# Halves of an activation next to each other, a shared last scaling, and reordered beginnings of two attention layers

## The chip, the cores and the metric

The kernel runs on one core of a Trainium2 chip. The metric is the time on the device in microseconds (us): the median of several runs. The kernel before takes 1296.48 us (three runs, 1295.65 to 1296.82). A row of the profile names the engines: PE is TensorE, PEld its weight load, DVE is VectorE, ACT is ScalarE, POOL is GpSimd and SP is SyncE, which issues nearly all DMAs.

## The reference, cut to what matters

Two blocks on 256 tokens of width 1024, in fp32, one after the other. The first has four layers (a0, b0, c0, a1), each of which projects h, mixes tokens, gates, projects back and normalises:

```python
for i in range(DEPTH):                    # 4
    if kind == 0:                         # layers a
        branch = fourier_mix(h)
    elif kind == 1:                       # layer b: grouped-query attention
        q = apply_axial_rope(rms_norm(q, q_norm_g[j]), ang_row, ang_col)
        k = apply_axial_rope(rms_norm(k, k_norm_g[j]), ang_row, ang_col)
        branch = gqa_block_attention(q, k, v)
    else:                                 # layer c: three dilated windows, 16 heads
        qg = apply_rope(qkv[:, :, 0, g], ang_1d)
        kg = apply_rope(qkv[:, :, 1, g], ang_1d)
        og, lg = dilated_group_attention(qg, kg, qkv[:, :, 2, g], dil, window // (2 * dil))
        ...
    mem_out = memory_attention(qm, mk, mv)
    y = jnp.concatenate([branch, mem_out], axis=-1) * jax.nn.silu(gate)
    h = layer_norm(DEEPNORM_ALPHA * h + jnp.matmul(y, w_out[i]), ln_g[i], ln_b[i])
```

The second has two layers (d0, d1) of three mixers and an MLP, and a last norm:

```python
for l in range(DEPTH_2):                  # 2
    x = x + mix @ w_out[l]
    x = x + squared_relu_mlp(rmsnorm(x, norm_mlp_g[l]), mlp_w1[l], mlp_w2[l])
return rmsnorm(x, final_norm_g)
```

## The kernel before, in words

**Products in three parts.** An fp32 product is made of three matmuls on operands that are split into a high part, rounded, and a low part, the rest: high times high, high times low and low times high (mm3, L490 to L492). Activations are held with their features on the partitions: h_hi and h_lo, each 8 tiles (k) of 256 tokens, both in the tile h_both; r_hi and r_lo hold what goes into the projections back. Where a token tile of h is the stationary operand (token_major, chunks of queries and keys, residual), 128 of its columns are loaded and 512 columns of a weight stream. Where a weight is stationary (feature_major, feature_half), 256 tokens of h stream.

**The up products of the MLP (L1500, L1501)** do it in two matmuls: the high weights meet h_hi and h_lo in one matmul of 512 moving columns, and the low weights meet h_hi in one of 256. For each MLP there are 16 units with 16 such pairs, so each line runs 512 times in the kernel. In h_both the low half of a tile k lies 8 KB behind its high half.

**Weights** come in units of up to 1 MB. SP loads a unit into one of three raw slots, ACT rounds it (w_hi, L1603), DVE subtracts (w_lo, L2169), and PE waits for w_lo. There are three split slots, so ACT may round unit u when PE has finished unit u - 3. Which unit ACT and DVE take at which place is fixed by the calls round_weights(key, ahead) and weights(key, ahead): they handle all units up to the one that key's product uses, plus ahead (plus one in ACT's).

**Order.** There is no scheduler at run time: each engine runs the list that its block writes (block.tensor, block.scalar, block.vector, block.sync), and semaphores, wrapped in Steps, tie them together. Every wait is thus in front of all that stands behind it on its engine.

**Layer b, beginning.** PE: chunk 2 (keys and values), chunk 0 (first half of the queries), the memory queries (qm), heads(0), which is pair_scores(0) alone, half a chunk 1, turn_k, heads(1), the other half, gate 4, turn_q(0), and then heads(2), which starts with pair_turned(0). DVE: norms of the keys, rope_k twice, norms of the queries, then the calls that the diff reorders: rope_q rotates 8 heads of a token tile with sines (L2433) and cosines, pair_max(q) takes the row maxima of scores (L2457), for which the exponentials of ACT wait, pair_normal(q) divides by the sums (L2468), and weights(...) splits units. ACT: the exponentials of pair 0, the evacuations of turn_k (L1614), the rounding of the next unit, the exponentials of pair 1, tokens(1) (four reads of chunk 1, L1774 and L1775), two roundings, the silu of gate 4 (L1806), the evacuations of turn_q(0) (L1614), and those of pair_turned(0).

**Layer c, first section.** qk_section(0) has three chunks in six half chunks of one unit and 24 matmuls each. DVE rotates each finished chunk (rope) into the one tile c_rot (a part of prob, L2535), and PE transposes it from there (turn, through banks 3 and 6; the transposes are L578), after which ACT copies it out and DVE may rotate the next. The turns stand in front of half chunks 3 and 5 and in front of the second half unit of v_section(0).

**The end.** The last two products each add a half of a row tile to x (L2651), ACT sums the squares (L1992), rms makes the factor with small DVE instructions, and DVE scales a whole row tile by factor and gain in one instruction (L3023). SP stores a row tile when it is scaled (L1580).

Of the kernel before, what the change touches and what calls it, by code (L numbers as in the profile page):

```python
# [23 lines left out]
F32 = mybir.dt.float32  # L24
# [6 lines left out]
P = 128  # L31
# [119 lines left out]
def build(nc, A, out):  # L151
    _, n_kept = constants()
    with ExitStack() as ctx:
# [7 lines left out]
        h_both = sb("h_both", [P, 2, KT, S], F32R)  # L161
        h_hi, h_lo = h_both[:, 0, :, :], h_both[:, 1, :, :]
# [112 lines left out]
        row_out = Steps("row_out")  # L275
        vector_step = Steps("vector_step")
# [145 lines left out]
        C_TURN_BANK = (3, 6)  # L422
        C_EARLY_BANKS = (0, 1, 2, 4, 5)
# [55 lines left out]
        def _(pe):  # L479
# [264 lines left out]
            for li, (kind, j) in enumerate(LAYERS):  # L744
# [248 lines left out]
                else:  # L993
# [130 lines left out]
                    def qk_section(c):  # L1124
                        for i in range(6):
                            heads("qk", c, i)
                            if i in (3, 5):
                                turn(c, i // 2 - 1)
                            half_chunk(c, i)

                    def v_section(vh, turned, before):
                        for i in range(6):
                            heads("v", vh, i)
                            if i == before:
                                turn(turned, 2)
                            half_values(vh, i)
# [5 lines left out]
                    v_section(0, 0, 1)  # L1142
# [10 lines left out]
                    v_section(1, 2, 1)  # L1153
# [57 lines left out]
            for l in range(2):  # L1211
# [272 lines left out]
                def up(e):  # L1484
                    for u in range(2):
# [7 lines left out]
                        for k0 in range(0, KT, step):  # L1493
                            if e + u == 0:
                                pe.wait_ge(h_ready.sem, h_ready.at(((L, "mlp"), k0 // 2)))
                            for m in range(2):
                                o = bank[2 * u + m]
                                for k in range(k0, k0 + step):
                                    hi, lo = [a[:, k, m * P:(m + 1) * P] for a in w]
                                    nc.tensor.matmul(o, hi, h_both[:, :, k, :], start=k == 0, stop=False)  # L1500
                                    i = nc.tensor.matmul(o[:, 0:S], lo, h_hi[:, k, :], start=False, stop=k == KT - 1)  # L1501
                            if e + u + k0 == 0:
                                stream_tiles((L, "mlp"), (L, "wo"), 1)
# [22 lines left out]
        def _(sp):  # L1526
# [51 lines left out]
            for b in range(NB):  # L1578
                sp.wait_ge(row_out.sem, row_out.at(b))
                sp.dma_start(out[0, b * P:(b + 1) * P, :], z[:, b, :]).then_inc(stored, 16)  # L1580
            sp.wait_ge(stored, 16 * NB)
# [14 lines left out]
        def _(act):  # L1596
# [22 lines left out]
            def hidden_hi(L, nxt, tiles, tiles_there):  # L1619

                for j in range(4):
                    act.wait_ge(tiles_there.sem, tiles_there.at((L, "zt", j)))
                    nc.scalar.activation(flat2(h_hi[:, 2 * j:2 * j + 2, :]), tiles[:, j % 2, :], ACT.Copy)\
                        .then_inc(h_rounded.sem, h_rounded.next((nxt, j)))
# [68 lines left out]
            for j, what in ((1, "scaled"), (0, "hi"), (1, "hi"), (3, "scaled"), (2, "hi"), (3, "hi")):  # L1693
# [6 lines left out]
                else:  # L1700
                    there = tiles_scaled if j % 2 else tiles_read
                    act.wait_ge(there.sem, there.at(("in", "zt", j)))
                    nc.scalar.activation(flat2(h_hi[:, 2 * j:2 * j + 2, :]), tile_place(j), ACT.Copy).then_inc(h_rounded.sem, h_rounded.next(("a0", j)))
# [9 lines left out]
            for li, (kind, j) in enumerate(LAYERS):  # L1713
# [126 lines left out]
                else:  # L1840
# [66 lines left out]
                    def qk_section(c):  # L1907
                        for i in range(6):
                            heads("qk", c, i, turned=(c, i // 2 - 1) if i in (3, 5) else None)

                    def v_section(vh, turned, before):
                        for i in range(6):
                            heads("v", vh, i, turned=(turned, 2) if i == before else None)
# [11 lines left out]
                    v_section(0, 0, 1)  # L1925
# [13 lines left out]
                    v_section(1, 2, 1)  # L1939
# [213 lines left out]
            for n in range(2):  # L2153
                for b in range(NB):
                    act.wait_ge(dve_read.sem, dve_read.at(("d1", "dn", n, b)))
                    half_squares("end", "end", b, n)


        @block.vector
        def _(dve):  # L2160
# [49 lines left out]
            def first_tiles():  # L2210
# [8 lines left out]
                for j in range(4):  # L2219
# [4 lines left out]
                    v.tensor_tensor(flat2(h_lo[:, pair, :]), tile_place(j), flat2(h_hi[:, pair, :]).bitcast(F32), SUB).then_inc(h_ready.sem, h_ready.next(("a0", j)))  # L2224
# [152 lines left out]
            for li, (kind, j) in enumerate(LAYERS):  # L2377
# [33 lines left out]
                elif kind == "b":  # L2411
# [13 lines left out]
                    def rope(b, c0, nh, gain, rot, rs):  # L2425
# [5 lines left out]
                        for r in range(2):  # L2431
                            for f in range(2):
                                tt(r5[:, :, f, r, :], s5[:, :, f, 1 - r, :], t5[:, f, r, :].unsqueeze(1).to_broadcast([P, nh, 16]), MUL)  # L2433
# [48 lines left out]
                    norms(8, 8, ("p", 0), b_sq, "qm")  # L2482
                    rope_q(0, 0)
                    pair_max(0)
                    weights((L, "s", 0, 1))
                    rope_q(0, 1)
                    pair_normal(0)
                    pair_max(1)
                    weights((L, "s", 1, 1))
# [173 lines left out]
            for l in range(2):  # L2663
# [306 lines left out]
                def tile_lo(part, j):  # L2970
# [3 lines left out]
                    v.tensor_tensor(flat2(h_lo[:, pair, :]), split_t[:, j % 2, :], flat2(h_hi[:, pair, :]).bitcast(F32), SUB)\  # L2974
# [41 lines left out]
                for n in range(2 if l == 1 else 0):  # L3016
                    for b in range(NB):
                        add_rows((L, "dn", n, b), n, b, bank[4 + 2 * n + b], factor=S_(10 + b, 1))
                        if n == 1:
                            link(rms("end", "end", b))  # L3020
                            if b == 0:
                                dve.wait_ge(gf_loaded, 16)
                            v.scalar_tensor_tensor(z[:, b, :], x[:, b, :], S_(8 + b, 1), gf, MUL, MUL).then_inc(row_out.sem, row_out.next(b))  # L3023
# [25 lines left out]
```

## Time and profile before

| what | value |
|---|---|
| median of three runs | 1296.48 us |
| the profiled execution | 1295.2 us |
| its span | 1293.4 us |
| PE busy | 1255.6 us (97%) |
| DVE busy | 892.0 us (69%) |
| ACT busy | 704.8 us (54%) |
| matmuls | 7512 |
| L1500 / L1501 | 512 matmuls each, mean 399 / 281 ns |
| from HBM | 194.94 MB, mean 152 GB/s with what is written |

The span is what the profile covers. The execution's time holds 1.8 us more, around it. Busy times of PE add up the durations of matmuls that overlap by their drains, so the distance between two starts tells the rate, and not the duration. An idle time in brackets stands in front of the row's first instruction, with the engine and line that ended it. A row with x8 merges eight instructions.

### The profile page before, as it was taken

How to read it: one execution, taken by the hardware profiler on the slowest of the kernel's cores; microseconds unless marked ns; L12 is line 12 of the kernel's file. 1: busy time of each engine (PE TensorE's matmuls, PEld its weight loads, DVE VectorE, ACT ScalarE, POOL GpSimd, SP SyncE). 2: the span in 40 equal slices, each digit the busy share in tenths (PEclk: the TensorE clock that was granted, in tenths of full speed). 3: DMA queues.
4: the chain of work that ended last, by engine and by line, in shares of the span. 5: the costliest groups of instructions: out<-in, count | busy, mean ns of one | idle time of the engine just before them, and what ended most of it. 6: DMA issues, size and time to landing. Idle time of an engine off the chain costs nothing.

```text
span 1293.4 us, 19153 instructions
## 1 busy us (share of the span) xinstructions
PE 1255.6 (97%) x7512; PEld 1073.4 (83%) x7512; DVE 892.0 (69%) x1602; ACT 704.8 (54%) x1029; POOL 2.4 (0%) x8
## 2 busy tenths in 40 slices
PE   8999999999999999999999999999999999999997
PEld 7997787778888787887998987888888987888885
DVE  6677996685664746547566998766657897766655
ACT  5634577453467565575535676544444676544442
POOL 0000000000000000000000000000000000000000
PEclk9999999999999999999999999999999999999999
DMA  9444532445643335333343454455654544456560
GB/s 275 148 168 140 163 116 82 163 163 163 196 163 114 119 127 163 98 112 125 115 157 109 150 167 134 138 193 191 200 191 131 170 142 136 148 182 209 184 223 32
DMA packets 147054, 197.22 MB, mean 152 GB/s; under 512 B 4732, under 2 KB 102294, under 8 KB 146966
## 3 DMA queue, kind: packets, MB, share of 16 engines
q1 hardware_dynamic: 146838, 195.96, 47.0%
q8 instruction: 60, 0.98, 0.3%
q14 instruction: 28, 0.23, 0.1%
q0 software_dynamic: 128, 0.04, 0.0%
HBM read 194.94 MB, written 1.05 MB: 152 GB/s over the span
## 4 chain that ended last, share of the span: by engine, by line
PE 79%; DVE 12%; ACT 5%; issue 3%; DMA 0%; DVEq 0%; ACTq 0%
PE bank L490 18%; PE bank L492 17%; PE bank L491 17%; PE bank L1500 9%; PE bank L1501 5%; PE bank L578 4%; DVE w_lo L2169 3%; DVE stat L2189 2%; PE bank L1073 1%; PE bank L787 1%; PE bank L691 1%; ACT w_hi L1603 1%; PE bank L1110 1%; DVE stat L2186 1%; DVE arena L2183 1%
## 5 line engine op out<-in xcount | busy, mean ns | idle before, releaser
L2169 DVE TENSOR_TENSOR w_lo<-w_raw,w_hi 128x2048 fp32r<-128x2048 f32 (+5 forms) x190 | 412.9, 2182 | 132.2 <-ACT w_hi L1603 129.5
L1603 ACT ACTIVATE w_hi<-w_raw 128x2048 fp32r<-128x2048 f32 (+5 forms) x190 | 346.3, 1829 | 231.0 <-PE bank L492 157.6
L490 PE MATMUL bank<-w_hi,r_hi 128*128 128x512 f32 (+3 forms) x536 | 207.7, 387 | 2.6 <-DVE w_lo L2169 2.4
L492 PE MATMUL bank<-w_hi,r_lo 128*128 128x512 f32 (+3 forms) x536 | 204.3, 381 | 0.0
L491 PE MATMUL bank<-w_lo,r_hi 128*128 128x512 f32 (+3 forms) x536 | 204.0, 381 | 0.0
L1500 PE MATMUL bank<-h_both,w_hi 128*128 128x512 f32 x512 | 182.0, 399 | 2.0 <-DVE h_both L2974 2.0
L490 PE MATMUL bank<-w_hi,h_both 128*128 128x512 f32 (+3 forms) x464 | 178.4, 384 | 1.8 <-DVE w_lo L2169 1.0
L492 PE MATMUL bank<-w_hi,h_both 128*128 128x512 f32 (+3 forms) x464 | 174.6, 376 | 0.0
L491 PE MATMUL bank<-w_lo,h_both 128*128 128x512 f32 (+3 forms) x464 | 174.4, 376 | 0.0
L1501 PE MATMUL bank<-h_both,w_lo 128*128 128x256 f32 x512 | 143.7, 281 | 0.0
L490 PE MATMUL bank<-h_both,w_hi 128*128 128x256 f32 x464 | 133.9, 289 | 2.1 <-DVE w_lo L2169 2.1
L491 PE MATMUL bank<-h_both,w_hi 128*128 128x256 f32 x464 | 131.2, 283 | 0.0
L492 PE MATMUL bank<-h_both,w_lo 128*128 128x256 f32 x464 | 131.1, 283 | 0.0
L490 PEld LDWEIGHTS bank<-w_hi,r_hi 128*128 128x128 f32 x536 | 100.7, 188 | 23.0 <-DVE w_lo L2169 3.1
L1500 PEld LDWEIGHTS bank<-h_both,w_hi 128*128 128x128 f32 x512 | 96.2, 188 | 26.9 <-DVE h_both L2974 1.8
L492 PEld LDWEIGHTS bank<-w_hi,r_lo 128*128 128x128 f32 x536 | 100.7, 188 | 19.6
L491 PEld LDWEIGHTS bank<-w_lo,r_hi 128*128 128x128 f32 x536 | 100.8, 188 | 17.5
L490 PEld LDWEIGHTS bank<-w_hi,h_both 128*128 128x128 f32 x464 | 87.2, 188 | 19.5 <-issue 2.6
L492 PEld LDWEIGHTS bank<-w_hi,h_both 128*128 128x128 f32 x464 | 87.1, 188 | 14.9
L491 PEld LDWEIGHTS bank<-w_lo,h_both 128*128 128x128 f32 x464 | 87.3, 188 | 13.4
L1501 PEld LDWEIGHTS bank<-h_both,w_lo 128*128 128x128 f32 x512 | 96.7, 189 | 0.5
L490 PEld LDWEIGHTS bank<-h_both,w_hi 128*128 128x128 f32 x464 | 88.8, 191 | 8.1 <-issue 7.4
(304 smaller groups left out, 1608.6 us busy)
## 6 DMA issues: line engine op xcount, KB each, us to landing
w_raw<-in_mlp_w SPq DMA_DIRECT2D x64, 1024.0 KB, 5.4
w_raw<-in_w_out SPq DMA_DIRECT2D x24, 1024.0 KB, 5.1
w_raw<-in_w_in_c SPq DMA_DIRECT2D x48, 512.0 KB, 4.5
w_raw<-in_w_in_c SPq DMA_DIRECT2D x18, 1024.0 KB, 5.1
w_raw<-in_w_in_a SPq DMA_DIRECT2D x12, 1024.0 KB, 7.2
w_raw<-in_w_in_b SPq DMA_DIRECT2D x12, 1024.0 KB, 5.1
w_raw<-in_w_in SPq DMA_DIRECT2D x8, 1024.0 KB, 5.3
w_raw<-in_w_out SPq DMA_DIRECT2D x8, 512.0 KB, 3.7
```

What stands on the lines that cost most here:

```text
L490: nc.tensor.matmul(o, lhs[0], rhs[0], start=start, stop=False)
L491: nc.tensor.matmul(o, lhs[0], rhs[1], start=False, stop=False)
L492: return nc.tensor.matmul(o, lhs[1], rhs[0], start=False, stop=stop)
L578: i = nc.tensor.transpose(o[0:a.shape[1], n * width:n * width + P], a, ident)
L691: nc.tensor.matmul(bank[2 * n + b][:, j * P:(j + 1) * P], h_part, ident_r[:], start=j + part == 0, stop=False)
L787: i = nc.tensor.matmul(o[:, c * S + c0:c * S + c1], spectra[:, b, t, c, part, :], tables[b][part if c == 0 else 2 * part], start=b == 0, s ...
L1073: m = nc.tensor.matmul(bank[4 + par][:, c0:c1], cqT[rows, n, p % 4, qs], ckT[rows, n, p % 4, ks], start=True, stop=True)
L1500: nc.tensor.matmul(o, hi, h_both[:, :, k, :], start=k == 0, stop=False)
L1501: i = nc.tensor.matmul(o[:, 0:S], lo, h_hi[:, k, :], start=False, stop=k == KT - 1)
L1603: nc.scalar.activation(w_hi[:, u % SPLIT_SLOTS, 0:kts * n], w_raw[:, u % RAW_SLOTS, 0:kts * n], ACT.Copy).then_inc(w_rounded.sem, w_rounde ...
L2169: v.tensor_tensor(w_lo[:, s, 0:m], w_raw[:, u % RAW_SLOTS, 0:m], w_hi[:, s, 0:m].bitcast(F32), ALU.subtract)\
L2189: link(v.scalar_tensor_tensor(o, a, s, b, op0, op1))
```

## The change

Four edits. In the tile h_both, the two halves of a tile k now lie next to each other, and L1500 reads them as one run; the writers of h_hi and h_lo write two runs of 256. In layer b, rope multiplies both f at once, pair_max(0) stands in front of rope_q(0, 0), and the split after the second scores stands in front of pair_normal(0). In layer c, the turns of section 0 stand in front of half chunk 4 and in front of the units 0 and 2 of v_section(0). At the end, the first half of the last row tile is multiplied by the gain (final_norm_g, in gf) before its factor is known, ACT multiplies that half by the factor while DVE scales the other, and SP stores the two halves by themselves.

```diff
-        h_both = sb("h_both", [P, 2, KT, S], F32R)
-        h_hi, h_lo = h_both[:, 0, :, :], h_both[:, 1, :, :]
+        h_both = sb("h_both", [P, KT, 2, S], F32R)
+        h_hi, h_lo = h_both[:, :, 0, :], h_both[:, :, 1, :]
...
+        C_TURN_AT = ((4,), (3, 5))
...
                     def qk_section(c):
                         for i in range(6):
                             heads("qk", c, i)
-                            if i in (3, 5):
-                                turn(c, i // 2 - 1)
+                            if i in C_TURN_AT[c > 0]:
+                                turn(c, C_TURN_AT[c > 0].index(i))
                             half_chunk(c, i)
 
                     def v_section(vh, turned, before):
                         for i in range(6):
                             heads("v", vh, i)
-                            if i == before:
-                                turn(turned, 2)
+                            if i in before:
+                                turn(turned, 3 - len(before) + before.index(i))
                             half_values(vh, i)
...
-                    v_section(0, 0, 1)
+                    v_section(0, 0, (0, 2))
...
-                                    nc.tensor.matmul(o, hi, h_both[:, :, k, :], start=k == 0, stop=False)
+                                    nc.tensor.matmul(o, hi, h_both[:, k, :, :].rearrange("p a s -> p (a s)"), start=k == 0, stop=False)
...
-            for b in range(NB):
-                sp.wait_ge(row_out.sem, row_out.at(b))
-                sp.dma_start(out[0, b * P:(b + 1) * P, :], z[:, b, :]).then_inc(stored, 16)
-            sp.wait_ge(stored, 16 * NB)
+            sp.wait_ge(row_out.sem, row_out.at(0))
+            sp.dma_start(out[0, 0:P, :], z[:, 0, :]).then_inc(stored, 16)
+            sp.wait_ge(half_out.sem, half_out.at(1))
+            sp.dma_start(out[0, P:S, 0:512], z[:, 1, 0:512]).then_inc(stored, 16)
+            sp.wait_ge(row_out.sem, row_out.at(1))
+            sp.dma_start(out[0, P:S, 512:], z[:, 1, 512:]).then_inc(stored, 16)
+            sp.wait_ge(stored, 16 * 3)
...
+            act.wait_ge(end_scale.sem, end_scale.at(1))
+            nc.scalar.activation(z[:, 1, 0:512], z[:, 1, 0:512], ACT.Copy, scale=S_(9, 1)).then_inc(half_out.sem, half_out.next(1))
...
                         for r in range(2):
-                            for f in range(2):
-                                tt(r5[:, :, f, r, :], s5[:, :, f, 1 - r, :], t5[:, f, r, :].unsqueeze(1).to_broadcast([P, nh, 16]), MUL)
+                            tt(r5[:, :, :, r, :], s5[:, :, :, 1 - r, :], t5[:, :, r, :].unsqueeze(1).to_broadcast([P, nh, 2, 16]), MUL)
...
                     norms(8, 8, ("p", 0), b_sq, "qm")
+                    pair_max(0)
                     rope_q(0, 0)
-                    pair_max(0)
                     weights((L, "s", 0, 1))
                     rope_q(0, 1)
+                    weights((L, "s", 1, 1))
                     pair_normal(0)
                     pair_max(1)
-                    weights((L, "s", 1, 1))
                     pair_normal(1)
...
                 for n in range(2 if l == 1 else 0):
+                    if n == 1:
+                        dve.wait_ge(gf_loaded, 16)
+                        dve.wait_ge(square_sum.sem, square_sum.at(("end", "end", 1, 0)))
+                        v.tensor_tensor(z[:, 1, 0:512], x[:, 1, 0:512], gf[:, 0:512], MUL)
                     for b in range(NB):
                         add_rows((L, "dn", n, b), n, b, bank[4 + 2 * n + b], factor=S_(10 + b, 1))
                         if n == 1:
-                            link(rms("end", "end", b))
-                            if b == 0:
-                                dve.wait_ge(gf_loaded, 16)
-                            v.scalar_tensor_tensor(z[:, b, :], x[:, b, :], S_(8 + b, 1), gf, MUL, MUL).then_inc(row_out.sem, row_out.next(b))
+                            cols = slice(512 * b, D)
+                            rms("end", "end", b).then_inc(end_scale.sem, end_scale.next(b))
+                            dve.wait_ge(end_scale.sem, end_scale.at(b))
+                            v.scalar_tensor_tensor(z[:, b, cols], x[:, b, cols], S_(8 + b, 1), gf[:, cols], MUL, MUL).then_inc(row_out.sem, row_out.next(b))
```

Left out are the two new semaphores, the writers of h_hi and h_lo whose source is now seen as two runs (as in `tiles[:, j % 2, :].rearrange("p (m s) -> p m s", m=2)`), and ACT's calls that follow the turns of PE.

## Rows read from the trace of the kernel before

**Rows 1.** A stretch of the first MLP (busy us per engine), and the page's chain of waits.

```profile
811.00:990.00 179.00, 178.02 (x904) 150.60 (x904) 115.94 (x114) 82.46 (x75) 0.00 (x0) 1.00 0.56 180
...
PE 79%; DVE 12%; ACT 5%; issue 3%; DMA 0%; DVEq 0%; ACTq 0%
```

**Rows 2.** PE in order of time: start, duration, line; last, L1500 on the page.

```profile
165.29 0.28 PE L491 MATMUL bank<-h_both,w_hi 128*128 128x256 f32 x1
...
170.80 0.28 PE L492 MATMUL bank<-h_both,w_lo 128*128 128x256 f32 x1
...
870.08 0.28 PE L1501 MATMUL bank<-h_both,w_lo 128*128 128x256 f32 x1
...
880.32 0.28 PE L1501 MATMUL bank<-h_both,w_lo 128*128 128x256 f32 x1
...
881.61 0.39 PE L492 MATMUL bank<-w_hi,r_lo 128*128 128x512 f32 x1
...
889.79 0.39 PE L492 MATMUL bank<-w_hi,r_lo 128*128 128x512 f32 x1
...
L1500 PE MATMUL bank<-h_both,w_hi 128*128 128x512 f32 x512 | 182.0, 399 | 2.0 <-DVE h_both L2974 2.0
```

**Rows 3.** PE in order of time, the spatial product of layer d0.

```profile
779.19 1.16 PE L1357 MATMUL bank<-gate,const 128*128 128x128 f32 x8
```

**Rows 4.** PE in order of time, the waits in the beginning of layer b.

```profile
157.46 0.88 PE L909 MATMUL bank<-mem_kv,arena 64*128 64x256 f32 x5 [1.31 <-ACT prob L1798]
...
165.10 0.36 PE L490 MATMUL bank<-h_both,w_hi 128*128 128x256 f32 x1 [0.84 <-DVE w_lo L2169]
...
172.35 1.12 PE L578 MATMUL bank<-const,prob 128*128 128x128 f32 x8 [0.39 <-ACT arena L1614]
```

**Rows 5.** DVE in order of time, pair_max(0) and pair_max(1) of layer b.

```profile
153.32 1.29 DVE L2457 TENSOR_REDUCE stat<-bank 128x2 f32<-128x512 f32 x2
...
161.48 1.28 DVE L2457 TENSOR_REDUCE stat<-bank 128x2 f32<-128x512 f32 x2
```

**Rows 6.** ACT in order of time, from tokens(1) to the evacuations of turn_q(0).

```profile
165.97 3.76 ACT L1603 ACTIVATE w_hi<-w_raw 128x2048 fp32r<-128x2048 f32 x2
169.75 1.28 ACT L1806 ACT_TABLE_LOAD   x1
...
171.62 1.08 ACT L1614 ACTIVATE arena<-bank 128x512 f32<-128x512 f32 x2
```

**Rows 7.** Groups of DVE by shape, 118 to 205 us: count, busy us, mean ns.

```profile
L2183 DVE TENSOR_TENSOR arena<-arena 128x128 f32<-128x128 f32 x16 | 4.6, 290 | 0.4
...
L2235 DVE TENSOR_TENSOR h_both<-split_t,h_both 128x256 fp32r<-128x256 f32 x6 | 2.5, 420 | 0.3 <-ACT h_both L1634 0.2
...
L2183 DVE TENSOR_TENSOR arena<-arena 128x256 f32<-128x256 f32 x4 | 1.7, 425 | 0.1
```

**Rows 8.** DVE, ACT and PE in order of time, the beginning of layer c.

```profile
271.09 4.49 DVE L2169 TENSOR_TENSOR w_lo<-w_raw,w_hi 128x2048 fp32r<-128x2048 f32 x2 [1.38 <-ACT w_hi L1603]
...
280.61 2.29 DVE L2169 TENSOR_TENSOR w_lo<-w_raw,w_hi 128x2048 fp32r<-128x2048 f32 x1
...
273.63 1.92 ACT L1603 ACTIVATE w_hi<-w_raw 128x2048 fp32r<-128x2048 f32 x1 [0.80 <-PE bank L492]
...
280.68 0.95 PE L578 MATMUL bank<-const,prob 128*128 128x128 f32 x7 [1.50 <-DVE prob L2535]
```

**Rows 9.** The end in order of time, SP's first issues, and DMA issues with us to landing.

```profile
1289.05 1.29 DVE L3023 SCALAR_TENSOR_TENSOR arena<-arena,stat,gate 128x1024 f32<-128x1024 f32 x1
...
1286.44 0.63 ACT L1992 ACTIVATE arena<-arena 128x512 f32<-128x512 f32 x1 [3.87 <-DVE arena L2651]
...
2.15 7.99 SPq L1544 DMA_DIRECT2D arena<-in_x  x16
...
const<-in_const SPq DMA_DIRECT2D x1, 64.0 KB, 2.0
...
out<-arena SPq DMA_DIRECT2D x2, 512.0 KB, 2.7
```

More of the change, by code:

```diff
@@ L275, in build @@
         row_out = Steps("row_out")
+        end_scale = Steps("end_scale")
+        half_out = Steps("half_out")
         vector_step = Steps("vector_step")
@@ L1152, in _ @@
                     qk_section(2)
-                    v_section(1, 2, 1)
+                    v_section(1, 2, (1,))
                     qk_section(3)
@@ L1622, in hidden_hi @@
                     act.wait_ge(tiles_there.sem, tiles_there.at((L, "zt", j)))
-                    nc.scalar.activation(flat2(h_hi[:, 2 * j:2 * j + 2, :]), tiles[:, j % 2, :], ACT.Copy)\
+                    nc.scalar.activation(h_hi[:, 2 * j:2 * j + 2, :], tiles[:, j % 2, :].rearrange("p (m s) -> p m s", m=2), ACT.Copy)\
                         .then_inc(h_rounded.sem, h_rounded.next((nxt, j)))
@@ L1702, in _ @@
                     act.wait_ge(there.sem, there.at(("in", "zt", j)))
-                    nc.scalar.activation(flat2(h_hi[:, 2 * j:2 * j + 2, :]), tile_place(j), ACT.Copy).then_inc(h_rounded.sem, h_rounded.next(("a0", j)))
+                    nc.scalar.activation(h_hi[:, 2 * j:2 * j + 2, :], tile_place(j).rearrange("p (m s) -> p m s", m=2), ACT.Copy).then_inc(h_rounded.sem, h_rounded.next(("a0", j)))
             round_unit(3)
@@ L1908, in qk_section @@
                         for i in range(6):
-                            heads("qk", c, i, turned=(c, i // 2 - 1) if i in (3, 5) else None)
+                            heads("qk", c, i, turned=(c, C_TURN_AT[c > 0].index(i)) if i in C_TURN_AT[c > 0] else None)
                     def v_section(vh, turned, before):
                         for i in range(6):
-                            heads("v", vh, i, turned=(turned, 2) if i == before else None)
+                            heads("v", vh, i, turned=(turned, 3 - len(before) + before.index(i)) if i in before else None)
                             if i % 2:
@@ L1924, in _ @@
                     qk_section(0)
-                    v_section(0, 0, 1)
+                    v_section(0, 0, (0, 2))
                     qk_section(1)
@@ L1938, in _ @@
                     qk_section(2)
-                    v_section(1, 2, 1)
+                    v_section(1, 2, (1,))
                     qk_section(3)
@@ L2156, in _ @@
                     half_squares("end", "end", b, n)
+            for b in range(NB):
+                end_scale.at(b)
+            act.wait_ge(end_scale.sem, end_scale.at(1))
+            nc.scalar.activation(z[:, 1, 0:512], z[:, 1, 0:512], ACT.Copy, scale=S_(9, 1)).then_inc(half_out.sem, half_out.next(1))
         @block.vector
@@ L2223, in first_tiles @@
                     dve.wait_ge(h_rounded.sem, h_rounded.at(("a0", j)))
-                    v.tensor_tensor(flat2(h_lo[:, pair, :]), tile_place(j), flat2(h_hi[:, pair, :]).bitcast(F32), SUB).then_inc(h_ready.sem, h_ready.next(("a0", j)))
+                    v.tensor_tensor(h_lo[:, pair, :], tile_place(j).rearrange("p (m s) -> p m s", m=2), h_hi[:, pair, :].bitcast(F32), SUB).then_inc(h_ready.sem, h_ready.next(("a0", j)))
                 dve.wait_ge(h_ready.sem, h_ready.made)
@@ L2973, in tile_lo @@
                     dve.wait_ge(h_rounded.sem, h_rounded.at((part, j)))
-                    v.tensor_tensor(flat2(h_lo[:, pair, :]), split_t[:, j % 2, :], flat2(h_hi[:, pair, :]).bitcast(F32), SUB)\
+                    v.tensor_tensor(h_lo[:, pair, :], split_t[:, j % 2, :].rearrange("p (m s) -> p m s", m=2), h_hi[:, pair, :].bitcast(F32), SUB)\
                         .then_inc(h_ready.sem, h_ready.next((part, j)))
```

## The prediction

> **What bounds the kernel now.** I read the page first, then the chain of waits, then TensorE (PE) in order of time, and last the three places that the diff touches. PE is busy nearly without a gap: in a stretch of the first MLP it works 178.0 of 179 us at full clock, while VectorE (DVE) has 116, ScalarE (ACT) 82 and the DMA engines a share of 0.56, and the chain that ended last is PE for 79% [rows 1]. So a step counts only if it shortens PE's stream, takes away one of PE's few waits, or lies in the tail after PE's last product. What remains beside the stream in the places of the diff is four waits of PE, 1.31, 0.84, 0.39 and 1.50 us [rows 4, 8], and the tail behind the last row scaling [rows 9].
>
> **Step 1, halves side by side (L1500).** The line streams 512 columns, 256 of h_hi and 256 of h_lo. They lie 8 KB apart before and side by side after; nothing else about the 512 matmuls changes. The busy time of a matmul includes its drain, so I take the distance between starts. Pure 512-column matmuls: 881.61 to 889.79 holds 36 of them, 227.2 ns each. Pure 256-column ones: 165.29 to 170.80 holds 46, 119.8 ns each. Both are the columns at 2.4 GHz plus about 13.5 ns. A pair of L1500 and L1501 takes (880.32 - 870.08) / 29 = 353.1 ns, which is 6.1 ns more than 227.2 + 119.8 = 347.0 [rows 2]. The only thing that L1500 has and the others have not is the break in its moving operand, so I give the 6.1 ns to the break. Times 512 that is 3.1 us. About 0.2 us of it is swallowed at the beginnings of the two MLPs, where PE waits for h_both anyway (2.0 us in all, last row of [rows 2]). Term: -2.9 us. Bounds: 0 (the alternation of long and short matmuls costs the 6.1 ns, not the break) and -4.5 us (L1501 keeps its own short distance, near 117 ns, and L1500 falls from 236 to 227). A second place where a moving operand has two runs is L1357: eight passes take 1.16 us against 1.12 for eight of L578, both with a delayed first one [rows 3, 4], so 5 ns a pass. That is why I stay near the middle.
>
> The Trainium skill (SBUF — State Buffer, "Door 1: The DMA port swizzle", the note on cachelines) says that reads run at full rate while consecutive accesses share a 16-byte line. Runs of 256 fp32 elements and of 512 walk the same lines, so by that rule the break costs nothing and this term is 0; it is the first rival below.
>
> The writers of h_both now write two runs of 256 instead of one of 512 (four activations and four subtractions at each border). L2235 does so already with runs of 128, and its 256 elements take 420 ns against 425 ns for the 256 of L2183 [rows 7]. I put 0, with 0.1 us a border either way.
>
> **Step 2, layer b (grouped-query).** rope multiplies with two DVE instructions of 256 elements instead of four of 128. A 128-element one takes 290 ns, a 256-element one 425 ns [rows 7], and some 40 ns pass between them: 1.32 becomes 0.93, so 0.4 us less for each rope_q. Each rope_k (four of 64 into two of 128) gives as much, but the split of the next unit then waits for ACT's rounding, and I keep 0.2 us of it.
>
> Next the order. Before, pair_max(0) stands behind rope_q(0, 0), at 153.32 [rows 5]; PE's second scores wait 1.31 us for the exponentials that hang on it [rows 4]. Moved ahead, it starts some 3.5 us earlier, behind the norms, and that wait goes. The split of the unit for gate 4 stands behind pair_max(1) before, and PE waits 0.84 us for it [rows 4]; moved ahead of pair_normal(0), it is done before PE asks. Taken alone these are -2.15 us.
>
> But the split of 2.2 us (half of the 4.49 that two take in the first row of [rows 8]) now stands in front of pair_max(1). That starts at 161.48 before [rows 5] and at 161.48 + 2.2 - 0.8 (two rope_q) - 0.2 = 162.7 after, 1.2 us later. ACT does everything that follows in written order: exp(1), the four reads of tokens(1), two weight roundings (3.76 us), a table load (1.28), the silu of gate 4, and then the evacuations of turn_q, from 171.62 [rows 6]. It has no idle time in that stretch, and only then has pair_turned(0) its banks; PE waits for just that, 0.39 us before 172.35 [rows 4]. All of it shifts by 1.2 us, to 173.5. PE arrives 2.15 us earlier and waits 0.39 + 2.15 + 1.2 = 3.7 us there. So the two waits do not vanish, they gather in one, and the layer is 1.2 us longer. DVE is not late afterwards (rope_q(1, 0) gives it 0.4 back, and by my count it starts pair_max(2) within 0.1 us of before), but PE has no gap behind in which to recover. Term: +1.2 us. Bounds: -2.15 us (the chain of ACT does not hold) and +2.2 us (the shorter rope gives nothing at pair_max(1)).
>
> **Step 3, layer c (dilated), first section.** PE stands 1.50 us before turn(0, 0) until DVE has rotated the first chunk (280.68, [rows 8]). After, half chunk 3 comes first. Its weights are split by 275.6 (two splits from 271.09), so PE goes on at 279.2, runs 24 matmuls of 227 ns (5.5 us), and turns at 284.6, 4 us after the rotation is done. What could be late next: the unit of half chunk 4 is rounded from 273.63 and split from 280.61 to 282.9 [rows 8], and PE needs it at 285.5. The unit of half chunk 5 is now rounded as soon as half chunk 2 is done (near 279.1, before it stood behind the evacuations of the turn) and split by about 285, for 290.9. The second rotation must wait for turn(0, 0) to leave c_rot, starts at about 285.5 instead of 286.5, and its turn comes at 296. The moves into v_section (0 and 2 instead of 1) leave DVE 5 us for the third rotation. The number of turns is the same, and each bank that PE opens there was read before. Term: -1.5 us. Bounds: -1.5 and 0 (a unit late by as much).
>
> **Step 4, the tail.** Before, the last scaling takes 1.29 us on 1024 columns, from 1289.05, then SP issues one store of 512 KB (2.7 us from issue to landing, [rows 9]). After, half of the row is multiplied by the gain beforehand, in DVE's gap before its last additions, so it costs nothing. DVE then scales 512 columns and ACT the other 512 at the same time. ACT takes about 0.63 us for 512 (the squares, [rows 9]; no table load is due for a copy), so both halves are ready at 1289.8 instead of 1290.35. Two stores leave instead of one: 16 issues took 7.99 us at the beginning, 0.5 each [rows 9], so the second goes at about 1290.3. It carries 256 KB, between the 64 KB that landed in 2.0 us and the 512 KB in 2.7: 2.3 us, end 1292.6 against 1293.05. Term: -0.5 us; bounds -0.8 (2.0 to landing) and -0.1 (2.7).
>
> **Sum.** -2.9 + 1.2 - 1.5 - 0.5 = -3.7 us. The profiled execution took 1295.2 us (span 1293.4 and 1.8 around it), so one like it would take 1291.5. It is 1.3 us faster than the median of the runs, 1296.48, to which I carry the difference: 1292.8 us, 0.29% less.
>
> **Rivals.**
> A, the break is free: what a pair of L1500 and L1501 loses is the price of a long matmul next to a short one. For it: the row of L1357 is thin, and no other stretch alternates lengths. Against it: 256 and 512 columns carry the same fixed part where they stand alone [rows 2]. Then -0.8 us: 1295.7. The rule of the Trainium skill cited at step 1 leads to the same result.
> B, layer b keeps its gain: ACT works faster than its order in [rows 6] suggests and PE's two waits simply go. For it: this is what the two moves act on. Against it: the 0.39 us wait, already there, with ACT full in front of it. Then -2.9 - 2.15 - 1.5 - 0.5 = -7.0: 1289.4.
> C, a unit of weights is late in layer c, and the wait of 1.50 us comes back at another instruction: -2.2, 1294.3. Against it: 2.6 us of room at half chunk 4.
> D, slower: single tiles of h_hi and h_lo now lie 2 KB apart instead of 1 KB, and every product of the layers reads them, 6 x 464 = 2784 matmuls at L490 to L492. Each nanosecond there costs 2.8 us, so it decides from 2.3 ns on (3.7 + 2.6 us); with 3 ns the kernel takes 1292.8 + 8.4 = 1301.2 us. Against it: the moving weights of those lines lie 2 KB apart already and run at 227.2 ns with 512 columns [rows 2].
>
> **Chances.** Forecast 0.60, A 0.15, B 0.12, C 0.08, D 0.05. Runs of this kernel tell about 0.2% (2.6 us) from no change. Faster by more than that: nine tenths of the forecast (it has a spread of about 1 us, and 1293.9 is where 0.2% ends) and B, 0.66. Within it: the rest of the forecast, A and C, 0.29. Slower: D, 0.05. The range goes from just under B to just over A, 1289.2 to 1295.9; the forecast's own, 1291.3 to 1294.3.
>
> **What would show it.** Step 1: the distance of an L1500/L1501 pair falls from 353 to 347 ns; if it stays, A. Step 2: no wait before the second scores and before gate 4, and one of about 3.7 us before the first transposes of prob at L578, released by ACT's evacuation; the distance from layer b's first product to its last 1.2 us longer. If that wait stays under 1 us, B. Step 3: no wait before the first turn of layer c and none new up to 310. Step 4: from the last statistics (1289.0) to the end 3.9 us instead of 4.4. What makes the forecast wrong most easily is a break that is free, or ACT's stretch in layer b being shorter than I count.

## The result, and the profile after

The changed kernel takes 1299.05 us (median of 20 runs, 1297.47 to 1300.55) against 1296.78 us of the kernel before (20 runs, 1295.22 to 1298.37): the ratio is 1.0022, 95% interval 1.0016 to 1.0027. It is slower by 2.3 us, where 3.7 us less were predicted. Each run also has its mean granted clock of TensorE, and this moves with the time. In 11 of the 20 runs it is 0.993 and they take 1299.96 us in the mean; 5 at 0.994 take 1298.72; 4 at 0.995 take 1297.62. The kernel before was granted 0.998 in its profiled run and 0.9967 as the mean of its runs beside the experiments. The profiled run of the changed kernel is one of the four at 0.995: it took 1297.55 us, 2.35 more than the profiled run before. Medians, ratios and mean clocks below leave out two runs that were far slower than all others, one of the kernel before (1386.73 us) and one of e8 (3181.73 us).

PE's order of time comes first (start, duration, line; the idle time and what ended it in brackets). These are the second scores, gate 4 and pair_turned(0) of layer b, then the first turn of layer c.

```profile
155.92 1.13 PE L912 MATMUL bank<-mem_kv,arena 64*128 64x256 f32 x8
...
162.57 0.28 PE L493 MATMUL bank<-h_both,w_hi 128*128 128x256 f32 x1
...
173.48 1.46 PE L581 MATMUL bank<-const,prob 128*128 128x128 f32 x8 [4.12 <-ACT arena L1620]
174.86 2.08 PE L912 MATMUL bank<-arena 64*128 64x256 f32 x8
...
287.21 1.03 PE L581 MATMUL bank<-const,prob 128*128 128x128 f32 x8
```

The waits of 1.31 and 0.84 us [rows 4] are gone, and so is the one of 1.50 us in layer c [rows 8]. The 0.39 us has become 4.12, where 3.7 were forecast. All that is as predicted, within about 0.4 us. What stands beside it was not: the eight transposes take 1.46 us, against 1.12 for the same eight in [rows 4], and the scores behind them 2.08 us, against 1.13 for those at 155.92. The view by stretches says why (start and end, length, busy us of PE, PEld, DVE, ACT and POOL, PE's granted clock, DMA share, GB/s):

```profile
170.00:172.00 2.00, 0.00 (x0) 0.00 (x0) 1.90 (x4) 1.98 (x2) 0.00 (x0) 1.00 0.00 0
172.00:174.00 2.00, 0.52 (x5) 0.48 (x6) 1.93 (x4) 1.81 (x4) 0.00 (x0) 1.00 0.01 3
174.00:176.00 2.00, 2.00 (x11) 1.50 (x12) 1.79 (x3) 1.19 (x2) 0.00 (x0) 0.53 0.92 275
176.00:178.00 2.00, 2.00 (x13) 1.35 (x10) 0.95 (x2) 0.18 (x1) 0.00 (x0) 0.62 0.74 254
178.00:180.00 2.00, 2.00 (x19) 2.00 (x18) 2.00 (x2) 1.99 (x5) 0.00 (x0) 1.00 0.00 0
...
566.00:568.00 2.00, 2.00 (x13) 1.66 (x14) 0.00 (x0) 2.00 (x4) 0.00 (x0) 0.66 0.21 74
568.00:570.00 2.00, 2.00 (x11) 1.53 (x8) 1.21 (x3) 0.76 (x2) 0.00 (x0) 0.50 0.00 0
```

PE stands still through 170 to 172 and most of 172 to 174, and then works at 0.53 and 0.62 of full speed, that is mostly at 1.2 GHz in place of 2.4. In the kernel before, the granted clock is 1.00 in all of 172 to 178; its row for the stretch in which the changed kernel shows 0.53 is

```profile
174.00:176.00 2.00, 2.00 (x19) 1.67 (x16) 1.90 (x4) 0.11 (x1) 0.00 (x0) 1.00 1.05 352
```

There is a second slow stretch at 566 to 570, behind a wait of 1.65 us that the kernel before has too, without a slow stretch behind it:

```profile
565.40 1.27 PE L581 MATMUL bank<-const,prob 128*128 128x128 f32 x8 [1.65 <-ACT prob L1877]
```

The pairs of the MLP in PE's order of time, first and last of 29:

```profile
871.93 0.28 PE L1504 MATMUL bank<-h_both,w_lo 128*128 128x256 f32 x1
...
881.82 0.28 PE L1504 MATMUL bank<-h_both,w_lo 128*128 128x256 f32 x1
```

From first to last it is 9.89 us over 28 pairs, 353.2 ns a pair, against 353.1 [rows 2]. The page has for the chain of waits and for the line:

```profile
PE 79%; DVE 10%; ACT 6%; issue 3%; SPq 1%; DMA 0%; DVEq 0%; ACTq 0%
...
L1503 PE MATMUL bank<-h_both,w_hi 128*128 128x512 f32 x512 | 181.9, 399 | 2.0 <-DVE h_both L2983 2.0
```

PE is the chain for 79% as in [rows 1], and the line's mean is 399 ns as before.

Put together from distances between the same instructions in the two profiled runs: layer b +1.3 us by its order and +1.6 by the slow stretch, layer c -1.7 in its first section and +1.5 by the second slow stretch, the wait at the beginning of d1's input product +0.35, the tail -0.45, the start and the rest -0.2. That is +2.4, the difference of the spans (1295.8 against 1293.4).

### The profile page after: what moved, and what is told of

The parts are those of the page before. It is cut to its first block, busy times and chain, and to the rows that moved or that the text cites. A ratio compares the mean times of both kernels' runs of the same rounds, so it can differ in the third digit from the quotient of the medians.

```text
span 1295.8 us, 19145 instructions
## 1 busy us (share of the span) xinstructions
PE 1257.7 (97%) x7512; PEld 1075.1 (83%) x7512; DVE 890.6 (69%) x1591; ACT 705.7 (54%) x1030; POOL 2.4 (0%) x8
## 4 chain that ended last, share of the span: by engine, by line
PE 79%; DVE 10%; ACT 6%; issue 3%; SPq 1%; DMA 0%; DVEq 0%; ACTq 0%
PE bank L493 18%; PE bank L495 17%; PE bank L494 17%; PE bank L1503 9%; PE bank L1504 5%; PE bank L581 4%; DVE w_lo L2179 2%; DVE stat L2199 2%; PE bank L1076 1%; ACT w_hi L1609 1%; PE bank L790 1%; PE bank L694 1%; PE bank L1113 1%; DVE stat L2196 1%; PE bank L938 1%
```

## The experiments

The ratio is to the kernel before, measured beside each kernel on the same chip: e1 to e4 on one chip, e5 to e8 on a second, e9 and e10 on a third. "Clock" is the mean over the timed runs of the granted clock, for the kernels before 0.9967, 0.9967 and 0.9971 on the three chips. Columns on layer b are from one profiled run of each kernel. "Layer b" is the distance on PE from the last waiting transposes of layer b's beginning (121.33 before) to the wait near 201 us; before it is 80.33, after it 83.18.

| kernel | median, us | ratio (95%) | clock | layer b | wait at pair_turned(0) |
|---|---|---|---|---|---|
| before, three chips | 1296.55, 1296.94, 1296.12 | | 0.9967 to 0.9971 | 80.33 | 0.39 |
| e1 layer b alone | 1300.64 | 1.0028 (1.0018 to 1.0038) | 0.9945 | 84.13 | 4.14 |
| e2 e1, PE kept busy | 1298.87 | 1.0017 (1.0008 to 1.0026) | 0.9958 | 81.63 | 0.41 |
| e3 layer c alone | 1295.15 | 0.9985 (0.9977 to 0.9994) | 0.9965 | 80.38 | as before |
| e4 layout alone | 1295.68 | 0.9996 (0.9988 to 1.0005) | 0.9973 | 80.38 | as before |
| e5 after, ACT shorter | 1295.72 | 0.9992 (0.9984 to 1.0001) | 0.9957 | 81.39 | 2.33 |
| e6 after without layer b | 1293.55 | 0.9982 (0.9973 to 0.9990) | 0.9974 | 80.37 | as before |
| e7 after, pair_max(1) first | 1292.66 | 0.9970 (0.9959 to 0.9981) | 0.9970 | 78.24 | 0.39 |
| e8 e7, PE kept busy in c | 1292.28 | 0.9966 (0.9953 to 0.9979) | 0.9975 | 78.24 | 0.39 |
| e9 rope alone | 1295.70 | 0.9996 (0.9987 to 1.0005) | 0.9969 | 79.5 | 0.39 |
| e10 before, PE kept busy in c | 1295.84 | 0.9997 (0.9988 to 1.0006) | 0.9974 | as before | as before |

### One part at a time: e1, e3, e4

**e1**, the kernel before with the merged rope and the new order of layer b, nothing else:

```diff
                     norms(8, 8, ("p", 0), b_sq, "qm")
+                    pair_max(0)
                     rope_q(0, 0)
-                    pair_max(0)
                     weights((L, "s", 0, 1))
                     rope_q(0, 1)
+                    weights((L, "s", 1, 1))
                     pair_normal(0)
                     pair_max(1)
-                    weights((L, "s", 1, 1))
                     pair_normal(1)
```

> The kernel before with the edits of layer b alone (merged rope, pair_max(0) first, split of gate 4's unit ahead of pair_normal(0)). Theory T (order plus clock): pair_turned(0) starts 1.2 us later than before because ACT's fixed chain starts 1.2 us later, and PE's idle time of about 4 us in front of it is followed by a stretch at the lower granted clock which costs another 1.6 us: +2.8 us, about 1299.6 against 1296.8. Rival R1 (order alone, as predicted): +1.2 us. Rival R2 (the slow stretch is a matter of the other edits or of chance): +1.2 us and a granted clock of 1.00 from 174 to 178 us.

Layer b alone makes the kernel slower, 1.0028. PE in order of time and by stretches:

```profile
174.00 1.94 PE L578 MATMUL bank<-const,prob 128*128 128x128 f32 x8 [4.14 <-ACT arena L1614]
```

```profile
172.00:174.00 2.00, 0.00 (x1) 0.03 (x1) 1.97 (x3) 1.99 (x4) 0.00 (x0) 0.68 0.00 0
174.00:176.00 2.00, 2.00 (x10) 1.67 (x10) 1.90 (x4) 0.97 (x3) 0.00 (x0) 0.50 0.60 179
176.00:178.00 2.00, 2.00 (x9) 1.18 (x9) 0.40 (x1) 0.58 (x1) 0.00 (x0) 0.50 1.01 352
```

The same gap and the same fall. Here the clock falls while PE still stands, to 0.68 in 172 to 174, is 0.50 in both stretches behind it and 0.61 in 178 to 180. The layer is 3.8 us longer: 1.3 us until pair_turned(0) starts and 2.5 behind it. This profiled run is the slowest of e1's eight.

**e3**, the new turns of layer c alone (C_TURN_AT and v_section, as in the change):

> The kernel before with the turns of layer c's first section moved and nothing else. Theory T: -1.5 us, no wait at the first turn. Rival R3 (the move brings about the second slow stretch that the changed kernel shows near 566 us): -1.5 + 1.6, no gain.

Its first section is 1.66 us shorter on PE (108.70 against 110.36 us from the layer's start to the wait near 375 us), and the kernel is faster, 0.9985. The interval holds the 1.5 us of the prediction.

**e4**, h_both with the halves side by side, alone:

```diff
-        h_both = sb("h_both", [P, 2, KT, S], F32R)
+        h_both = sb("h_both", [P, KT, 2, S], F32R)
```

> The kernel before with the new layout of h_both alone. Theory T (the break is free, a pair of L1500 and L1501 takes 353 ns in either layout): 0 us. Rival R4 (writers or readers of h pay for the layout somewhere): +0.5 us or more, spread over the borders of the layers.

No change that can be measured, 0.9996. PE in order of time, first and last of 32 pairs: 10.94 us over 31, 352.9 ns a pair.

```profile
871.06 0.28 PE L1501 MATMUL bank<-h_both,w_lo 128*128 128x256 f32 x1
...
882.00 0.28 PE L1501 MATMUL bank<-h_both,w_lo 128*128 128x256 f32 x1
```

### Is it the wait or the clock: e2, e5

**e2** is e1 with 16 matmuls of 512 columns, on constants and into a bank that is free, in front of heads(2). Their result is not used, and PE would stand still there otherwise:

```diff
                     turn_q(0)
+                    pe.wait_ge(*left[0])
+                    for _ in range(16):
+                        nc.tensor.matmul(bank[0][:, :], ident_r[:], dft_hi..., start=True, stop=True)
                     heads(2)
```

> e1_b_only with 16 matmuls of 512 columns into bank 0 between turn_q(0) and heads(2), whose results are overwritten; they fill PE's idle time in front of pair_turned(0) and use nothing that the other engines wait for. Theory T: the clock stays at 1.00, the start of pair_turned(0) stays where e1 has it, and the kernel gets back the 1.6 us of the slow stretch: +1.2 us against before, -1.6 us against e1. Rival R1 (the eight transposes and the scores are slow for another reason, such as a late evacuation or the port of PSUM): no change against e1, or slower by the matmuls.

PE in order of time and by stretches:

```profile
170.86 3.98 PE L965 MATMUL bank<-dft_hi,ident_r 128*128 128x512 f32 x16
175.26 1.12 PE L578 MATMUL bank<-const,prob 128*128 128x128 f32 x8 [0.41 <-ACT arena L1617]
```

```profile
172.00:174.00 2.00, 2.00 (x11) 1.59 (x10) 1.93 (x3) 1.98 (x2) 0.00 (x0) 1.00 0.00 0
174.00:176.00 2.00, 1.58 (x11) 1.07 (x10) 1.93 (x4) 1.67 (x5) 0.00 (x0) 1.00 0.08 13
176.00:178.00 2.00, 2.00 (x17) 1.45 (x16) 1.90 (x4) 1.01 (x2) 0.00 (x0) 1.00 0.97 309
```

The order of the work is that of e1, and pair_turned(0) starts as late as there (52.32 us behind layer b's beginning, 52.31 in e1). But the clock stays at 1.00, and the layer is 1.30 us longer than before, the size that was forecast, in place of 3.80. So the 1.3 us are the order and the 2.5 are the clock. By the medians the filled gap is worth 1.8 us (1300.64 to 1298.87), by the means 1.2 us (1300.15 to 1298.91); the two intervals in the table overlap, and the size in the timed runs is known only roughly. The kernel stays slower than before, as it must by the first term alone.

The kernel before holds the same device already: near 693 us its PE runs twelve matmuls of 512 columns on constants (3.05 us) in front of a wait of 0.62 us, with the clock at 1.00.

**e5** is the changed kernel, but ACT leaves the second of its two roundings in tokens(1) to heads(2), behind the evacuations:

```diff
-                        round_weights((L, "p", c, 1))
+                        round_weights((L, "p", c, 1), SPLIT_SLOTS - 1 if c == 1 else SPLIT_SLOTS)
```

> The changed kernel, but ACT rounds only one unit of weights behind tokens(1) and leaves the second to heads(2), where its list takes it anyway. Theory T (ACT's written order is what makes pair_turned(0) late): the evacuations of turn_q come 1.9 us earlier, the wait in front of pair_turned(0) falls from 4.1 to about 2.2 us, and the slow stretch behind it gets rarer or goes: 1.9 us under the changed kernel with the stretch, up to 3.5 us under it without. Rival (DVE's pair_max and norms are what is late, ACT only waits for them): no change against the changed kernel.

The wait shrinks by the 1.8 us of the rounding, and by the ratios the kernel gains 0.3% on the changed one. So what PE waits for is ACT's list, as the prediction had it. But 2.33 us are still enough for the clock to fall:

```profile
172.29 1.58 PE L581 MATMUL bank<-const,prob 128*128 128x128 f32 x8 [2.33 <-ACT arena L1620]
```

```profile
172.00:174.00 2.00, 1.71 (x10) 1.34 (x12) 1.97 (x3) 1.33 (x4) 0.00 (x0) 0.68 0.00 0
174.00:176.00 2.00, 2.00 (x9) 1.17 (x10) 1.90 (x4) 2.00 (x2) 0.00 (x0) 0.50 0.67 174
```

### What is left without layer b, and a better order: e6, e7

**e6** is the changed kernel with the rope and the order of layer b put back.

> The changed kernel with rope and the order of layer b as before: what is left are the layout, the turns of layer c and the shared last scaling. Theory T: 0 - 1.6 - 0.5 = -2.1 us against before, 1294.5. Rival (the loss is not in layer b's edits alone): same as before or slower.

It is faster than the kernel before, 0.9982, and its clock is back at 0.9974. The three waits of [rows 4] are there again (1.32, 0.83, 0.39), and the clock is 1.00 behind each. Its profiled run has one slow stretch, behind the wait of 1.65 us. So layer b's edits alone turn a gain of 0.2% into a loss of 0.2%.

**e7** keeps the early pair_max(0) and puts pair_max(1) in front of the split as well:

```diff
                     rope_q(0, 1)
+                    pair_max(1)
                     weights((L, "s", 1, 1))
                     pair_normal(0)
-                    pair_max(1)
                     pair_normal(1)
```

> The changed kernel with one more move: pair_max(1) stands directly behind rope_q(0, 1), ahead of the split of gate 4's unit and of pair_normal(0). Theory T: exp(1) starts near 160 us, ACT's chain ends by 169, the split is done at 162.6, in time for gate 4, and PE reaches pair_turned(0) at 169.7 with a wait under 1 us: layer b is 2.6 us shorter than before, and with layer c and the tail -4.7 us, 1292. Rival (DVE becomes the bound behind, because the norms of chunk 1 and the next splits are not earlier): the gain in layer b is given back by the third or fourth scores, -2 us in all, 1294.5.

With e8, which adds only idle work to it, this is the fastest kernel here: 1292.66 us (six runs, 1291.78 to 1293.26), 0.9970 of the one before, and by the ratios 0.5% faster than the changed one. DVE, ACT and PE in order of time:

```profile
160.95 1.29 DVE L2466 TENSOR_REDUCE stat<-bank 128x2 f32<-128x512 f32 x2
162.15 2.28 DVE L2179 TENSOR_TENSOR w_lo<-w_raw,w_hi 128x2048 fp32r<-128x2048 f32 x1
...
165.47 3.74 ACT L1609 ACTIVATE w_hi<-w_raw 128x2048 fp32r<-128x2048 f32 x2
...
171.09 1.08 ACT L1620 ACTIVATE arena<-bank 128x512 f32<-128x512 f32 x2
...
171.83 1.12 PE L581 MATMUL bank<-const,prob 128*128 128x128 f32 x8 [0.39 <-ACT arena L1620]
```

pair_max(1) starts at 160.95. Counted from layer b's beginning (122.90 here, 121.19 in the changed kernel) that is 3.4 us earlier than in the changed kernel. The split behind it ends at 164.4, and gate 4 starts at 164.58, less than 0.3 us later than it could. Of the three waits one is left (0.39 us), and layer b takes 78.24 us, 2.1 less than before: the -2.15 that the prediction gave for the two waits without their consequence.

### The second slow stretch, and the small wait in d1: e8, e9, e10

**e8** is e7 and **e10** the kernel before, each with 6 such matmuls in front of the one pair_turned(q + 1) in the tail of layer c where the wait of 1.65 us is:

```diff
                     pair_values(q)
+                    pe.wait_ge(*left[3])
+                    for _ in range(6):
+                        nc.tensor.matmul(bank[3][:, :], ident_r[:], dft_hi..., start=True, stop=True)
                     pair_turned(q + 1)
```

> e7 with six matmuls of 512 columns into bank 3 in front of the pair_turned near 564 us, where PE waits 1.65 us for ACT in every version; their results are overwritten. Theory T (a slow stretch of the clock begins now and then where PE has just waited, and costs 1.6 us when it does): no slow stretch near 566 us, and a median 0.5 to 1 us under that of e7. Rival (the slow stretches come anyway, at whatever place): the same median as e7.

> The kernel before with the six matmuls into bank 3 in front of the pair_turned near 564 us. Theory T (a slow stretch that begins there now and then costs 1.6 us): the fastest runs stay at 1295.0 to 1295.5, and the median comes down by 0 to 0.8 us, toward them. Rival (the slow stretches only move to another of PE's waits, or the matmuls delay the transposes): median 1296.6 or more.

Neither can be told from its partner (0.9966 beside 0.9970 with four and six runs, and 0.9997): the gain of 0.5 to 1 us that was expected of e8 is not shown. No slow stretch stands near 566 us in their profiled runs. It doesn't stand there in e3, e4, e5, e7, e9 and the kernel before either; it does in the changed kernel, e1, e2 and e6. The same wait is followed by the low clock in one profiled run and not in another, and what decides is open.

**A third place, which no edit touches.** Near 22.6 us, in the kernel's beginning, PE waits for a w_lo, and there the length of the wait goes with the clock. It is 1.08 to 1.68 us in the kernel before, the changed one, e1, e5, e6 and e9, and no slow stretch follows. It is 1.77 to 2.46 us in e2, e3, e4, e7, e8 and e10, and each of them is at 0.50 in 24 to 26. PE in order of time and one stretch, of the kernel before and then of e7:

```profile
22.55 0.39 PE L490 MATMUL bank<-w_hi,r_hi 128*128 128x256 f32 x1 [1.15 <-DVE w_lo L2169]
24.00:26.00 2.00, 2.00 (x20) 2.00 (x19) 1.93 (x5) 1.30 (x2) 0.00 (x0) 1.00 1.10 348
```

```profile
22.63 0.50 PE L493 MATMUL bank<-w_hi,r_hi 128*128 128x256 f32 x1 [2.13 <-DVE w_lo L2179]
24.00:26.00 2.00, 2.00 (x11) 2.00 (x11) 1.93 (x5) 1.70 (x3) 0.00 (x0) 0.50 1.10 350
```

Layer b begins at 121.2 to 121.8 us in the six without this stretch and at 122.9 to 123.4 in the six with it, 1.1 to 2.2 us later. The edits do not sort the two groups (e10 differs from the kernel before only near 565 us), so by these profiles it is a matter of the single run. How often it comes in the timed runs is not shown.

**e9** is the kernel before with the merged rope alone:

```diff
                         for r in range(2):
-                            for f in range(2):
-                                tt(r5[:, :, f, r, :], s5[:, :, f, 1 - r, :], t5[:, f, r, :].unsqueeze(1)..., MUL)
+                            tt(r5[:, :, :, r, :], s5[:, :, :, 1 - r, :], t5[:, :, r, :].unsqueeze(1)..., MUL)
```

> The kernel before with the merged multiplications of rope alone. Theory T: DVE reaches pair_max(0) 0.5 us and pair_max(1) 1.0 us earlier, both waits of PE in front of the second scores and of gate 4 shrink by about as much, and layer b from its first turn to the wait near 201 us gets 0.4 to 1.3 us shorter. Theory S (the 0.35 us that the first MLP's stage is longer in every version with the merged rope belongs to it, by way of DVE's shorter list): the stage from the first to the second MLP's layer takes 194.3 instead of 193.95 us. Rival: layer b as before, since ACT's chain sets pair_turned(0) there too.

PE's waits at the second scores and at gate 4 go from 1.31 to 0.87 and from 0.84 to 0.46: 0.4 us for each rope, the size in the prediction, and 0.8 in the layer. In the kernel's time it can't be told from nothing. The wait for w_lo at the beginning of d1's input product, which was 0.47 us before and is 0.80 to 0.82 in the changed kernel and in all others that have both the merged rope and a new order, is 0.61 here. So it goes with layer b's edits, 850 us earlier; how is open.

## Why the prediction was wrong

Two things failed. Step 1 put 2.9 us on the break in the moving operand, and the break costs nothing. And the sum had no term for PE's clock behind the longer wait of step 2: it cost about 3 us. Together with 0.35 us at the wait in d1, for which there was no term either, this leads from -3.7 to about the +2.3 that was measured.

**What bounds the kernel** was read rightly: where a wait of PE was taken away alone (e3), the kernel became faster by about as much, and the rope's savings on DVE (e9) shortened layer b only by PE's two waits. What the reading left out is that the speed of PE's stream can change too.

**Step 1, -2.9 us: wrong, it is 0.** The pair takes 353.2 ns with the halves side by side, and 352.9 ns in e4. The 6.1 ns over the sum of the pure distances are there with and without the break. That they belong to a long matmul next to a short one, as rival A said, is what is left; no run here isolates it. The working's flaw: it subtracted distances of uniform sequences from that of an alternating one and gave the difference to the only feature left on its list, though the trace had no alternating sequence without a break to compare. The second support was none: the 1.16 us of L1357's eight passes lie inside what eight one-run passes of L578 take in the same trace, 1.03 to 1.27 us. The rule of the Trainium skill (SBUF — State Buffer, "Door 1: The DMA port swizzle", the note on cachelines) had it right, and the trace now agrees: 399 ns for the line in both kernels.

**Step 2, +1.2 us: right in mechanism and size of the order, and the clock's term was missing.** pair_max(1) starts at 162.68 us (162.7 was worked out). DVE and ACT of the changed kernel in order of time:

```profile
159.21 2.29 DVE L2179 TENSOR_TENSOR w_lo<-w_raw,w_hi 128x2048 fp32r<-128x2048 f32 x1
...
162.68 1.28 DVE L2466 TENSOR_REDUCE stat<-bank 128x2 f32<-128x512 f32 x2
```

```profile
163.46 0.47 ACT L1804 ACTIVATE prob<-bank,stat 128x256 f32<-128x256 f32 x1 [4.97 <-DVE stat L2466]
...
167.18 3.76 ACT L1609 ACTIVATE w_hi<-w_raw 128x2048 fp32r<-128x2048 f32 x2
170.95 1.28 ACT L1812 ACT_TABLE_LOAD   x1
172.25 0.60 ACT L1812 ACTIVATE gate<-bank 128x512 f32<-128x512 f32 x1
172.74 1.08 ACT L1620 ACTIVATE arena<-bank 128x512 f32<-128x512 f32 x2
```

ACT idles 4.97 us for the maxima and then runs its list without a gap, each step 1.1 to 1.2 us later than in [rows 6]; PE goes on at 173.48 (173.5 was worked out). Counted from layer b's beginning, which is 0.14 us earlier here, the order costs 1.27 us, and in e2 1.30. The prediction priced a wait of PE at its length. It did not ask what PE's clock does after it. Here the rows show the price: 1.6 us in the profiled runs of the changed kernel and of e5, 2.5 in that of e1, and none in e2, where PE was kept busy. The rule of the Trainium skill (TensorE: Matmul & The Clock Gate, "HAM oscillation — how this bites in real kernels") is that idle gaps of PE between bursts make the following burst start at the low clock. The rows agree (0.53 behind 4.12 us in the changed kernel), and the prediction should have weighed it.

**The size of the clock's part.** In the profiled run it can be read: two slow stretches, 1.6 and 1.5 us, 3.1 together. In the median it is only what is left over. The terms without the clock make -0.5 us (+1.3, -1.7, -0.45 and +0.35), and the medians differ by +2.3, so 2.8 us remain for it. Two things bear this out. The mean granted clock is 0.9937 against 0.9967 for the kernel before beside the experiments, and 0.003 of 1297 us are 3.9 us, part of it while PE stands still anyway. And at the same granted clock the changed kernel is not the slower one: its four runs at 0.995 take 1297.6 us in the mean, and the five of the kernel before at 0.995, on other chips, 1298.4. The clock has three decimals only, and one step of it is 1.3 us, so this comparison is rough. Which further slow stretch makes a run of 0.993 out of one of 0.995 is not shown, since timed runs leave no trace; the place near 22.6 us, free of one in the profiled run, is a candidate.

**Step 3, -1.5 us: right.** The first turn, at 287.21, has no wait, none is new, and the section is 1.66 us shorter, alone and in the whole; rival C did not happen.

**Step 4, -0.5 us: right.** ACT, DVE and SP in order of time, and the DMA issues:

```profile
1291.90 0.72 ACT L2166 ACTIVATE arena<-arena,stat 128x512 f32<-128x512 f32 x1 [1.89 <-DVE stat L2288]
```

```profile
1291.91 0.75 DVE L3036 SCALAR_TENSOR_TENSOR arena<-arena,stat,gate 128x512 f32<-128x512 f32 x1
```

```profile
1292.65 0.34 SPq L1584 DMA_DIRECT2D out<-arena  x1
1293.04 0.43 SPq L1586 DMA_DIRECT2D out<-arena  x1
```

```profile
out<-arena SPq DMA_DIRECT2D x2, 256.0 KB, 2.2
```

From the last statistics to the end of the span it is 3.9 us, against 4.35 before: 3.9 was worked out, with 2.3 us to landing where 2.2 came.

**The rivals.** A holds for step 1: the break is free. Its 1295.7 us still lie 3.4 us under the 1299.05 measured, for like the forecast it has no term for the clock or for the wait in d1. B (the waits simply go) is what e7's order gives, not the change's. D, the slower one, is refuted by e4: the three-part products of the layers run as before. The chance of slower, 0.05, stood for D alone. The slower case that came was not among the rivals, though its place was named: the gap of 3.7 us.

## What to carry to other kernels

Merging short waits of PE into one long one is not neutral: in layer b the waits of 2.33 to 4.14 us had the low clock behind them, and the short ones that they replaced had not. A run's mean granted clock, read beside its time, shows such a loss before any trace is opened. When a move helps one consumer, look for the reduction or exponential that an in-order engine then starts later, and follow that engine's list to PE's next bank; here the maxima belonged in front of the split. And a surplus worked out from mixed and uniform sequences is not yet due to a feature: first find a mixed sequence without it.

## What the runs showed of the hardware

- Around the end of PE's waits of 4.12, 4.14 and 2.33 us in layer b the granted clock fell to 0.50 to 0.68 for 4 to 6 us (three of three); behind waits of 1.35 us and less there it was 1.00. Near 22.6 us it fell behind waits of 1.77 to 2.46 us (six of six) and not behind 1.08 to 1.68 us (six of six). Behind the one of 1.65 us near 565 it fell in four of the ten profiled runs that have it unfilled. Further slow stretches stood near 604 to 612 (e3, e5, e9), where PE waits 1.4 us in every kernel; what decides at these last two places is open.
- Sixteen matmuls on constants in the gap of e1 (e2, 3.98 us) kept the clock at 1.00 and cost nothing: the work behind them started as late as without them (52.32 and 52.31 us behind the layer's beginning).
- A moving operand of 512 fp32 columns in two runs of 1 KB, 8 KB apart, streams as fast as one run of 2 KB (353.1 and 353.2 ns a pair).
- A pair of a 512-column and a 256-column matmul takes 6 ns more than the sum of what each takes among its own kind (353.2 against 347.0). What makes them is open.
